# The first norm's sum of squares as four one-column matmuls, and its reciprocal root as a row by two DMAs

## The chip, the core and the metric

The kernel runs on one core of a Trainium2 chip. The metric is the device time of one execution in microseconds, on the one core used. A core has five engines that run their own instruction streams and meet only at semaphores: TensorE (PE in the rows, with PEld for its weight loads), VectorE (DVE), ScalarE (ACT), GpSimd (POOL) and SyncE (SP). DMAs are issued by SP and, at a few places, by ScalarE's queue.

## The reference, cut to what matters

Two layers of one encoder block; 512 tokens, 1024 features, everything float32. Each layer begins with an RMS norm whose output feeds one wide input projection and, through it, four branches; the last step of a layer adds a gated embedding to the residual stream. The part that the change touches is the first norm of each layer:

```
def rms_norm(x, g):
    xf = x.astype(jnp.float32)
    y = xf * lax.rsqrt(jnp.mean(xf * xf, axis=-1, keepdims=True) + EPS)
    return (y * g.astype(jnp.float32)).astype(x.dtype)

for i in range(DEPTH):
    h = rms_norm(x, norm_g[i])
    proj = h @ w_in[i]
    (a_u, a_v, a_z, b_x, b_z, c_q, c_kv, c_kr, c_z,
     d_q, d_k, d_v, d_z, gates) = jnp.split(proj, split_at, axis=-1)
    ... four branches, gated, summed, projected, added to x ...
```

`c_q`, `c_kv`, `c_kr` (the latents) and `a_v` are normed again by their own norms, so a factor per token in front of them cancels but for the small epsilon.

## The kernel before, in words

The residual stream `x` lies transposed: features on the 128 partitions, 8 tiles of 128 features, 512 tokens in the free dimension. Every weight matrix comes in chunks of 128 x 1024 numbers (8 blocks of 128 x 128) through a ring of four slots: SP loads `w_raw`, ScalarE rounds it to `w_hi` (line 971), GpSimd subtracts to get `w_lo` (lines 464, 466; VectorE does this for the first four chunks), and TensorE multiplies in three float32r passes, high by high, high by low, low by high (`mm3`, lines 491 to 493; `first_rows`, lines 541 to 556, for the first four chunks of layer 0). The chunk order is the list `chunk_order`. The order on each engine is written out by hand, one function per engine and stage, and all meeting points are semaphores.

The first stage of a layer, `front(l)`, exists once per engine:

- The squares of x's tiles are made by ScalarE (`gained`, `n_sq`) and added up by VectorE into `n_acc` (lines 1348, 1351), 128 x 512: per partition, the sum over the 8 feature tiles. `n_summed` counts the additions. In layer 1 this happens at the end of layer 0's `tail`.
- TensorE multiplies chunks `lat0` to `lat3` (latents, token rows on partitions, 448 columns, banks 0 to 3) with the unnormed input times the gain (`act_hi`, `act_lo`), then `av0` to `av3` (banks 4 to 7). The missing factor r per token, one over the root of the mean square, is put in afterwards. Each chunk holds two of the eight feature tiles; in layer 0 each tile of a latent chunk is three groups of four matmuls in `first_rows`.
- Between `lat3` and `av0`, `norm_total` (lines 560 to 566) multiplies a 128 x 128 matrix of ones with `n_acc`, split into `n_hi` and `n_lo`: every partition of bank 7 then holds the total of each of the 512 tokens. Block 3 of `av0` writes bank 7, and so waits for `n_root` (`taken`).
- ScalarE makes the square root of all of bank 7 into `r_b`, 128 x 512 (line 1008); a root of one number stands ahead of it (line 1006), and its table load with it. Then it squares the latents out of banks 0 to 3 (lines 1011, 1012, eight instructions, with their sums), rounds chunk `av2`, and takes the latents' root (line 1017).
- VectorE (lines 1408 to 1448) splits `n_acc`; in layer 0 takes the constants (`constants_taken`, lines 1357 to 1367) and makes the column of rope frequencies (line 1416, `freq_made`); gets r as a column, token on the partition, from `r_b` by a product with the identity and a reduction (lines 1419, 1421) and a reciprocal (1423); scales the latents out of PSUM (lines 1430 to 1436, `lat_taken`); in layer 0 waits for a transpose by TensorE (line 514, inside `av1`; it waits for `freq_made` and `lat_taken`) and computes the rope angles (lines 1445, 1372 to 1381); and makes the reciprocal of the whole `r_b` (line 1448).
- Then comes the loop over the 8 tiles: VectorE `n_t` = x times gain times `r_b` (line 1453), ScalarE rounds it to `h_hi` (line 1024), VectorE subtracts to `h_lo` (line 1336, `h_made`). TensorE's first product with h is `bx3`, right behind `av3`, and waits for `h_made` of each tile k in turn. All later input projections use h.

ScalarE's order in `front` is: `weights_up_to` for `lat3`, `av0`, `av1`, the roots, the squares, weights `av2`, the latents' root, then (after `av0` has ended) weights `av3`, (after `av1`) weights `bx3`, and the eight roundings of h.

## Time and profile before

| | us |
|---|---|
| time before, median of 3 runs | 1358.57 (1358.22 to 1361.79) |
| the profiled execution's own time | 1358.55 |
| its span in the profile | 1356.8 |
| TensorE busy | 1350.7 (6401 matmuls) |
| VectorE busy | 699.5 |
| ScalarE busy | 560.5 |
| GpSimd busy | 606.1 |

The profile is of one execution. Its span runs from the first to the last instruction, so the time around it is 1.75 us. The granted TensorE clock is full over the whole span. A timeline row gives the start, the busy time, and the instruction with what it writes and reads; a matmul's busy time overlaps the next one's, so what a matmul costs is read from the distance between two starts. Square brackets give idle time of the engine before the row and what ended it.

### The profile page before, as it was taken

What the parts mean: (1) busy time and instruction counts of PE and PEld (TensorE: products, weight loads), DVE (VectorE), ACT (ScalarE), POOL (GpSimd) and SP (SyncE); (2) the same over time, 40 slices, a digit from 0 to 9 for tenths busy, and PEclk for the clock granted to TensorE, in tenths of its full rate; (3) what the DMA queues carried; (4) which work ended last, traced back from release to release, by engine and by line L of the source; (5) the groups of instructions that cost most, each with busy time, mean ns of one, the idle gap of its engine ahead of it and who ended that gap; (6) DMA issues with size and microseconds to landing.
All of it is one profiled execution on the core that took longest, in us unless ns stands there. A gap on an engine that the chain in (4) does not pass through costs nothing.

```text
span 1356.8 us, 16150 instructions
## 1 busy us (share of the span) xinstructions
PE 1350.7 (100%) x6401; PEld 1136.3 (84%) x6401; DVE 699.5 (52%) x1065; ACT 560.5 (41%) x870; POOL 606.1 (45%) x455
## 2 busy tenths in 40 slices
PE   9999999999999999999999999999999999999998
PEld 8788888888888888888888888888888888888887
DVE  7996445144553223265779955441445432343743
ACT  6365454255552222224444554443555322222242
POOL 3444252444434445445565542334333444544543
PEclk9999999999999999999999999999999999999999
DMA  7322222222222333323333222223222333333332
GB/s 209 92 86 94 63 79 74 90 86 85 87 79 93 93 100 102 109 93 96 99 108 94 85 94 63 78 75 97 78 79 81 90 95 104 97 93 109 100 101 95
DMA packets 68268, 126.32 MB, mean 93 GB/s; under 512 B 9040, under 2 KB 37984, under 8 KB 68192
## 3 DMA queue, kind: packets, MB, share of 16 engines
q1 hardware_dynamic: 66960, 124.72, 30.2%
q8 instruction: 51, 0.84, 0.3%
q10 hardware_dynamic: 1232, 0.55, 0.1%
q14 instruction: 25, 0.20, 0.0%
HBM read 123.15 MB, written 2.10 MB: 92 GB/s over the span
## 4 chain that ended last, share of the span: by engine, by line
PE 98%; DVE 1%; ACT 0%; issue 0%; DVEq 0%
PE ps L491 31%; PE ps L493 31%; PE ps L492 31%; PE ps L764 1%; PE ps L699 1%; PE ps L800 1%; PE ps L686 1%; PE ps L541 1%; PE ps L551 0%; DVE n_t L1453 0%; PE ps L556 0%; DVE h_lo L1336 0%; PE ps L582 0%; DVE r_b L1448 0%; PE ps L618 0%
## 5 line engine op out<-in xcount | busy, mean ns | idle before, releaser
L464 POOL TENSOR_TENSOR w_lo<-w_raw,w_hi 128x512 fp32r<-128x512 f32 x222 | 304.4, 1371 | 724.4 <-ACT w_hi L971 724.3
L491 PE MATMUL ps<-h_hi,w_hi 128*128 128x512 f32 (+1 forms) x1160 | 452.6, 390 | 1.0 <-DVE h_lo L1336 1.0
L493 PE MATMUL ps<-h_hi,w_lo 128*128 128x512 f32 (+1 forms) x1160 | 450.2, 388 | 0.0
L492 PE MATMUL ps<-h_lo,w_hi 128*128 128x512 f32 (+1 forms) x1160 | 449.9, 388 | 0.0
L971 ACT ACTIVATE w_hi<-w_raw 128x1024 fp32r<-128x1024 f32 x227 | 238.6, 1054 | 172.5 <-PE ps L493 166.5
L466 POOL TENSOR_TENSOR w_lo<-w_raw,w_hi 128x512 fp32r<-128x512 f32 x222 | 303.7, 1368 | 0.0
L491 PEld LDWEIGHTS ps<-h_hi,w_hi 128*128 128x128 f32 x1160 | 217.9, 188 | 46.6 <-DVE h_lo L1336 2.6
L493 PEld LDWEIGHTS ps<-h_hi,w_lo 128*128 128x128 f32 x1160 | 217.8, 188 | 45.1
L492 PEld LDWEIGHTS ps<-h_lo,w_hi 128*128 128x128 f32 x1160 | 217.9, 188 | 43.3
L1771 DVE SCALAR_TENSOR_TENSOR m_part<-th,ps 128x512 f32<-128x512 f32 x48 | 33.0, 687 | 237.9 <-PE ps L493 237.7
L1196 ACT ACTIVATE th<-ps 128x512 f32<-128x512 f32 x48 | 28.7, 597 | 183.5 <-PE ps L493 183.5
L491 PE MATMUL ps<-act_hi,w_hi 128*128 128x512 f32 x192 | 75.2, 392 | 0.0
L493 PE MATMUL ps<-act_hi,w_lo 128*128 128x512 f32 x192 | 74.8, 389 | 0.0
L492 PE MATMUL ps<-act_lo,w_hi 128*128 128x512 f32 x192 | 74.7, 389 | 0.0
L491 PE MATMUL ps<-m_hi,w_hi 128*128 128x512 f32 x128 | 49.8, 389 | 0.0
L492 PE MATMUL ps<-m_lo,w_hi 128*128 128x512 f32 x128 | 49.8, 389 | 0.0
L493 PE MATMUL ps<-m_hi,w_lo 128*128 128x512 f32 x128 | 49.8, 389 | 0.0
L493 PEld LDWEIGHTS ps<-act_hi,w_lo 128*128 128x128 f32 x192 | 36.0, 188 | 7.6
L492 PEld LDWEIGHTS ps<-act_lo,w_hi 128*128 128x128 f32 x192 | 36.1, 188 | 7.3
L491 PEld LDWEIGHTS ps<-act_hi,w_hi 128*128 128x128 f32 x192 | 36.1, 188 | 7.3
L1596 DVE SCALAR_TENSOR_TENSOR merged<-th_b,ps 128x512 f32<-128x512 f32 x16 | 11.0, 684 | 50.9 <-PE ps L493 50.9
L491 PE MATMUL ps<-w_hi,act_hi 128*128 128x512 f32 (+1 forms) x96 | 36.9, 384 | 0.0
(329 smaller groups left out, 1992.2 us busy)
## 6 DMA issues: line engine op xcount, KB each, us to landing
w_raw<-w_in SPq DMA_DIRECT2D x180, 512.0 KB, 3.5
w_raw<-w_in SPq DMA_DIRECT2D x92, 128.0 KB, 2.5
w_raw<-w_in SPq DMA_DIRECT2D x36, 256.0 KB, 3.0
x<-x_in SPq DMA_DIRECT2D x8, 256.0 KB, 4.1
w_raw<-w_in SPq DMA_DIRECT2D x32, 64.0 KB, 2.0
out_x<-x SPq DMA_DIRECT2D x7, 256.0 KB, 3.7
p_raw<-p_in SPq DMA_DIRECT2D x2, 512.0 KB, 4.4
w_raw<-w_in ACTq DMA_DIRECT2D x4, 128.0 KB, 3.0
```

The source lines that it names most:

```text
L464: pool.tensor_tensor(w_lo_t[s][:, 0:4, :], w_raw_t[s][:, 0:4, :], w_hi_t[s][:, 0:4, :].bitcast(F32), ALU.subtract)
L466: pool.tensor_tensor(w_lo_t[s][:, 4:8, :], w_raw_t[s][:, 4:8, :], w_hi_t[s][:, 4:8, :].bitcast(F32), ALU.subtract).then_inc(w_lo_made, 1)
L491: pe.matmul(o, a_hi, b_hi, start=first, stop=False, skip_group_check=skip)
L492: pe.matmul(o, a_hi, b_lo, start=False, stop=False, skip_group_check=skip)
L493: return pe.matmul(o, a_lo, b_hi, start=False, stop=last, skip_group_check=skip)
L541: pe.matmul(bank(t, LAT), act_hi[:, at_[t]], v_hi[:, u, 0:LAT], start=k == 0, stop=False)
L686: last = pe.matmul(ps[:, s:s + keys], q[at_, b * P:keys], k[at_, 0:keys], start=False, stop=q is qr_lo, skip_group_check=True)
L699: last = pe.transpose(ps[:, o:o + P], prob[:, i:i + P], ident[:])
L764: last = pe.transpose(ps[:, b * 512 + t * P:b * 512 + (t + 1) * P], i, ident[:])
L971: act.activation(w_hi_t[s][:, 0:n, :], w_raw_t[s][:, 0:n, :], ACT.Copy).then_inc(w_hi_made, 1)
L1196: act.activation(th[:, i % 4, :], bank(b), ACT.Tanh, scale=0.5).then_inc(g_tanh, 1)
L1771: dve.scalar_tensor_tensor(o, th[:, i % 4, :], 1.0, bank(b), ALU.add, ALU.mult).then_inc(y_taken, 1)
```

## The change

TensorE no longer multiplies a matrix of ones with the split sums. It takes each block of 128 tokens of `n_acc` (plain float32) as the stationary operand and one column of ones as the moving one, four matmuls with one output column each, into columns 0 to 3 of bank 7 (`norm_sums`): the totals now lie with the token on the partition. It does this one step earlier: in layer 0 before the last feature tile of `lat3`, in layer 1 before `lat3`. VectorE turns the four columns into mean plus epsilon (`v`), ScalarE takes the root of 4 columns in place of 512, and VectorE the reciprocal r. `av0` now waits as a whole for `n_var`. The product with the identity, the reduction, the split, the first small root and the 512-column reciprocal are gone. In layer 0 VectorE does `constants_taken` after r in place of before it.

The row that the h loop needs, r of every token on all partitions, comes from memory: ScalarE's queue issues a DMA that writes r's 128 x 4 numbers to a scratch row of 512 (between the latents' squares and chunk `av2`), and, after chunk `av3` and a wait for the first one to land, a DMA that reads that row into all 128 partitions of `r_b`. VectorE waits for it where the reciprocal of `r_b` was.

```diff
--- before.py
+++ after.py
@@ -85,7 +85,7 @@
                      ("kn", 1), ("kr", 1))
 CC, CONSTS = columns(("ident", P), ("ones", P), ("negtri", P), ("neg_i", P), ("mask_c", P), ("mask_d", P),
                      ("keep", 1), ("inv_edge", G * PAD), ("inv_win", G), ("freq", 1))
-SM, SMALL = columns(("eps_v", TB), ("root", TB), ("r", TB), ("lat_sum", 2 * TB), ("lat_root", 2 * TB),
+SM, SMALL = columns(("v", TB), ("eps_v", TB), ("root", TB), ("r", TB), ("lat_sum", 2 * TB), ("lat_root", 2 * TB),
                     ("lat_inv", 2 * TB), ("bn", 6 * TB), ("mv", 2 * TB), ("ln_root", TB), ("ln_inv", TB),
                     ("kr_sum", TB), ("qk_sum", 16), ("qk_root", 16), ("qk_inv", 16), ("rq", 8), ("neg_rq", 8),
                     ("top", 8), ("bias", 8), ("total", 8), ("inv_total", 8), ("pool_gain", G), ("ln_col", 2 * G))
@@ -183,8 +183,7 @@
 
 
         xb, trail_a, trail_b = plan(0, 13, ("xb", [G, WIN], F32), ("trail_a", [WIN], F32), ("trail_b", [WIN], F32))
-        n_sq, n_acc, on_diag = plan(24, 32, ("n_sq", [2, SEQ], F32), ("n_acc", [SEQ], F32), ("on_diag", [SEQ], F32))
-        n_hi, n_lo = plan(24, 28, ("n_hi", [SEQ], F32R), ("n_lo", [SEQ], F32R))
+        n_sq, n_acc = plan(24, 32, ("n_sq", [2, SEQ], F32), ("n_acc", [SEQ], F32))
         cqn_hi, cqn_lo, ckvn_hi, ckvn_lo = plan(
             24, 36, ("cqn_hi", [2, SEQ], F32R), ("cqn_lo", [2, SEQ], F32R), ("ckvn_hi", [SEQ], F32R),
             ("ckvn_lo", [SEQ], F32R))
@@ -256,6 +255,8 @@
         def sems(names):
             return [sem(n) for n in names.split()]
 
+        r_row = nc.dram_tensor("r_row", (DEPTH, SEQ), F32).ap()
+
         x_loaded = [sem(f"x_loaded{d}") for d in range(KD)]
         pos_loaded, par_loaded, const_loaded, rows_loaded, p_loaded, out_stored = sems(
             "pos_loaded par_loaded const_loaded rows_loaded p_loaded out_stored")
@@ -267,8 +268,8 @@
 
         ones_made, consts_made, rope_args, rope_sines, freq_made, freq_ready, freq_taken = sems(
             "ones_made consts_made rope_args rope_sines freq_made freq_ready freq_taken")
-        hx_hi_made, hx_made, n_squared, n_summed, n_split, n_total, n_root = sems(
-            "hx_hi_made hx_made n_squared n_summed n_split n_total n_root")
+        hx_hi_made, hx_made, n_squared, n_summed, n_total, n_var, n_root, r_made, r_stored, rb_loaded = sems(
+            "hx_hi_made hx_made n_squared n_summed n_total n_var n_root r_made r_stored rb_loaded")
         gain_diag, gain_ready, gain_taken, h_scaled, h_hi_made, h_made = sems(
             "gain_diag gain_ready gain_taken h_scaled h_hi_made h_made")
         lat_squared, lat_var, lat_root, lat_scaled, lat_taken, lat_ready, lat_hi_made, lat_made = sems(
@@ -500,7 +501,7 @@
                                k == KD - 1)
                 last.then_inc(done(l, name), 1)
 
-            def project_rows(l, name, i, hi, lo, b, n=SEQ, rope_frequencies=False, taken=None):
+            def project_rows(l, name, i, hi, lo, b, n=SEQ, rope_frequencies=False):
 
                 w_hi, w_lo = chunk(l, name)
                 v_hi = w_hi[:].rearrange("p (k s) c -> p k (s c)", k=2)
@@ -518,8 +519,6 @@
                         s = slice(k * SEQ + t * P, k * SEQ + (t + 1) * P)
                         if l and k == 0 and name.startswith("lat"):
                             pe.wait_ge(x_moved, after((l - 1) * KD + 4 + t))
-                        if taken and k == 0 and t == TB - 1:
-                            pe.wait_ge(*taken)
                         last = mm3(bank(b + t, n), hi[:, s], lo[:, s], v_hi[:, u, 0:n], v_lo[:, u, 0:n], k == 0,
                                    k == KD - 1)
                 last.then_inc(done(l, name), 1)
@@ -531,6 +530,8 @@
                 v_lo = w_lo[:].rearrange("p (k s) c -> p k (s c)", k=2)
                 for u in range(2):
                     k = 2 * c + u
+                    if c == 3 and u:
+                        norm_sums(0)
                     at_ = [slice(k * SEQ + t * P, k * SEQ + (t + 1) * P) for t in range(TB)]
                     pe.wait_ge(hx_hi_made, after(k))
                     if c == 0 and u == 0:
@@ -557,13 +558,17 @@
                                          stop=k == KD - 1)
                 last.then_inc(done(0, f"lat{c}"), 1)
 
-            def norm_total(l):
-
-                pe.wait_ge(n_split, after(l))
-                if l:
+            def norm_sums(l):
+
+                pe.wait_ge(n_summed, after(l * KD + KD - 1))
+                if l == 0:
+                    pe.wait_ge(ones_made, after(0))
+                else:
                     pe.wait_ge(gate_scaled, after(l * KD - 1))
-                pe.matmul(bank(7), ones_r[:], n_hi[:], start=True, stop=False)
-                pe.matmul(bank(7), ones_r[:], n_lo[:], start=False, stop=True).then_inc(n_total, 1)
+                for t in range(TB):
+                    last = pe.matmul(ps[:, 7 * 512 + t:7 * 512 + t + 1], tile(n_acc, t, P), ones[:, 0:1], start=True,
+                                     stop=True)
+                last.then_inc(n_total, 1)
 
             def rope_rows(l):
 
@@ -594,9 +599,11 @@
                     if l == 0:
                         first_rows(i)
                         continue
+                    if i == 3:
+                        norm_sums(l)
                     project_rows(l, f"lat{i}", i, hx_hi, hx_lo, 0, LAT)
-                norm_total(l)
-                project_rows(l, "av0", 0, hx_hi, hx_lo, 4, taken=(n_root, after(l)))
+                pe.wait_ge(n_var, after(l))
+                project_rows(l, "av0", 0, hx_hi, hx_lo, 4)
                 project_rows(l, "av1", 1, hx_hi, hx_lo, 4, rope_frequencies=l == 0)
                 project_rows(l, "av2", 2, hx_hi, hx_lo, 4)
                 rope_rows(l)
@@ -1003,20 +1010,24 @@
                 weights_up_to(l, "av0")
                 act.wait_ge(*end_of(l, "lat2"))
                 weights_up_to(l, "av1")
-                act.activation(sm("root", 0), eps[:], ACT.Sqrt)
-                act.wait_ge(n_total, after(l))
-                act.activation(r_b[:], bank(7), ACT.Sqrt, bias=eps[:], scale=1.0 / D_MODEL).then_inc(n_root, 1)
+                act.wait_ge(n_var, after(l))
+                act.activation(sm("root"), sm("v"), ACT.Sqrt).then_inc(n_root, 1)
                 act.wait_ge(*end_of(l, "lat3"))
                 for t in range(TB):
                     act.activation(lat_sq[:, t, 0:2 * P], bank(t, 2 * P), ACT.Square, accum_out=sm("lat_sum", t))
                     last = act.activation(lat_sq[:, t, 2 * P:3 * P], ps[:, t * 512 + 2 * P:t * 512 + 3 * P], ACT.Square,
                                           accum_out=sm("lat_sum", TB + t))
                 last.then_inc(lat_squared, 1)
+                act.wait_ge(r_made, after(l))
+                act.dma_start(r_row[l].rearrange("(t p) -> p t", p=P), sm("r"), allow_slow_non_contiguous=True).then_inc(
+                    r_stored, 16)
                 weights_up_to(l, "av2")
                 act.wait_ge(lat_var, after(l))
                 act.activation(sm("lat_root"), sm("lat_sum"), ACT.Sqrt).then_inc(lat_root, 1)
                 act.wait_ge(*end_of(l, "av0"))
                 weights_up_to(l, "av3")
+                act.wait_ge(r_stored, 16 * after(l))
+                act.dma_start(r_b[:], r_row[l].partition_broadcast(P)).then_inc(rb_loaded, 16)
                 act.wait_ge(*end_of(l, "av1"))
                 weights_up_to(l, "bx3")
                 for k in range(KD):
@@ -1406,21 +1417,19 @@
                                   0.5, None, ALU.mult)
 
             def front(l):
-                dve.wait_ge(n_summed, after(l * KD + KD - 1))
-                settle(dve.tensor_copy(n_hi[:], n_acc[:]))
-                low(n_lo[:], n_acc[:], n_hi[:]).then_inc(n_split, 1)
+                dve.wait_ge(n_total, after(l))
+                dve.tensor_scalar(sm("v"), ps[:, 7 * 512:7 * 512 + TB], 1.0 / D_MODEL, EPS, ALU.mult, ALU.add).then_inc(
+                    n_var, 1)
+                dve.wait_ge(n_var, after(l))
+                dve.tensor_scalar(sm("eps_v"), sm("v"), EPS, None, ALU.mult)
+                dve.wait_ge(n_root, after(l))
+                dve.reciprocal(sm("r"), sm("root")).then_inc(r_made, 1)
                 if l == 0:
                     constants_taken()
                     gain_rows(0)
                     dve.wait_ge(pos_loaded, 16 * (TB + 1))
                     dve.tensor_scalar(freq_b[:], ones[:], freq[:, G:G + 1], None, ALU.mult).then_inc(freq_made, 1)
-                dve.wait_ge(n_root, after(l))
-                by_block = on_diag[:].rearrange("p (t s) -> p t s", t=TB)
-                settle(dve.tensor_tensor(by_block, r_b[:].rearrange("p (t s) -> p t s", t=TB),
-                                         over(ident[:], [P, TB, P], 1), ALU.mult))
-                settle(dve.tensor_reduce(sm("root"), by_block, AXIS_X, ALU.add))
-                dve.scalar_tensor_tensor(sm("eps_v"), sm("root"), EPS, sm("root"), ALU.mult, ALU.mult)
-                settle(dve.reciprocal(sm("r"), sm("root")))
+                dve.wait_ge(r_made, after(l))
                 dve.wait_ge(lat_squared, after(l))
                 dve.scalar_tensor_tensor(sm("lat_sum", 0, TB), sm("lat_sum", 0, TB), 1.0 / (2 * P), sm("eps_v"),
                                          ALU.mult, ALU.add)
@@ -1445,7 +1454,7 @@
                     dve.tensor_copy(freq_row[:], ps[:, FREQ_AT:FREQ_AT + HALF]).then_inc(freq_taken, 1)
                     dve.wait_ge(freq_taken, after(0))
                     rope_angles()
-                settle(dve.reciprocal(r_b[:], r_b[:]))
+                dve.wait_ge(rb_loaded, 16 * after(l))
                 for k in range(KD + 1):
                     if k < KD:
                         if k > 1:

```

## Rows read from the trace of the kernel before

**Rows 1.** The page's chain that ended last, shares of the span by engine.
```profile
PE 98%; DVE 1%; ACT 0%; issue 0%; DVEq 0%
```

**Rows 2.** TensorE's waits over the whole span: total, times, longest us.
```profile
PE ps L491 <- DVE h_lo L1336: 1.0, 3, 0.4
```

**Rows 3.** Timeline of TensorE, layer 0, product bx3: start us, busy us, what.
```profile
49.55 0.39 PE L491 MATMUL ps<-h_hi,w_hi 128*128 128x512 f32 x1
...
52.61 0.50 PE L491 MATMUL ps<-h_hi,w_hi 128*128 128x512 f32 x1 [0.18 <-DVE h_lo L1336]
...
56.98 0.39 PE L491 MATMUL ps<-h_hi,w_hi 128*128 128x512 f32 x1
```

**Rows 4.** Timeline of TensorE, layer 1, the same product.
```profile
723.27 0.39 PE L491 MATMUL ps<-h_hi,w_hi 128*128 128x512 f32 x1
...
728.71 0.39 PE L491 MATMUL ps<-h_hi,w_hi 128*128 128x512 f32 x1
```

**Rows 5.** Timeline of VectorE, layer 0, what starts the scaled input.
```profile
35.56 0.19 DVE L1445 COPY freq_row<-ps 128x32 f32<-128x32 f32 x1 [0.82 <-PE ps L514]
...
39.32 3.34 DVE L1448 RECIPROCAL r_b<-r_b 128x512 f32<-128x512 f32 x1
42.70 1.41 DVE L1453 SCALAR_TENSOR_TENSOR n_t<-x,par,r_b 128x512 f32<-128x512 f32 x2
...
54.65 1.47 DVE L1336 TENSOR_TENSOR h_lo<-n_t,h_hi 128x512 fp32r<-128x512 f32 x2
```

**Rows 6.** Timeline of TensorE, layer 0, last latent chunk and the norm's total.
```profile
24.04 0.99 PE L541 MATMUL ps<-w_hi,act_hi 128*128 128x448 f32 x4
...
26.52 0.40 PE L565 MATMUL ps<-n_hi,ones_r 128*128 128x512 f32 x1
```

**Rows 7.** Timeline of VectorE, last sum of squares in layer 0 and layer 1.
```profile
21.31 0.68 DVE L1351 TENSOR_TENSOR n_acc<-n_acc,n_sq 128x512 f32<-128x512 f32 x1
...
691.66 0.68 DVE L1351 TENSOR_TENSOR n_acc<-n_acc,n_sq 128x512 f32<-128x512 f32 x1
```

**Rows 8.** Timeline of TensorE, short matmuls: ten transposes, then one float32 product.
```profile
152.57 1.25 PE L699 MATMUL ps<-ident,prob 128*128 128x128 f32 x10
...
153.90 0.39 PE L492 MATMUL ps<-act_lo,w_hi 128*128 128x512 f32 x1
...
43.75 0.49 PE L576 MATMUL ps<-gain_d,ones 128*128 128x128 f32 x2
...
44.31 0.39 PE L492 MATMUL ps<-w_lo,act_hi 128*128 128x512 f32 x1
```

**Rows 9.** Timeline of ScalarE, layer 0, around the root of the norm.
```profile
25.33 1.28 ACT L1006 ACT_TABLE_LOAD   x1
...
30.20 1.11 ACT L971 ACTIVATE w_hi<-w_raw 128x1024 fp32r<-128x1024 f32 x1
```

**Rows 10.** Timeline of VectorE, layer 0, constants and latents.
```profile
25.05 0.21 DVE L1359 COPY ident<-c_st 128x128 f32<-128x128 f32 x1
...
28.85 0.68 DVE L1419 TENSOR_TENSOR on_diag<-r_b,ident 128x512 f32<-128x512 f32 x1
...
31.44 0.20 DVE L1430 RECIPROCAL small<-small 128x8 f32<-128x8 f32 x1 [0.63 <-ACT small L1017]
...
33.42 0.41 DVE L1436 TENSOR_TENSOR krs<-ps,small 128x256 f32<-128x256 f32 x1
```

**Rows 11.** DMA issues by line over the span: KB each, median us to landing.
```profile
pos_i<-pos_in SPq DMA_DIRECT2D x4, 0.5 KB, 3.1
```

**Rows 12.** Timeline of layer 1: ScalarE's two weight casts, VectorE's first and last h tiles.
```profile
704.10 1.12 ACT L971 ACTIVATE w_hi<-w_raw 128x1024 fp32r<-128x1024 f32 x1
...
706.54 1.06 ACT L971 ACTIVATE w_hi<-w_raw 128x1024 fp32r<-128x1024 f32 x1 [1.23 <-PE ps L493]
...
712.07 1.42 DVE L1453 SCALAR_TENSOR_TENSOR n_t<-x,par,r_b 128x512 f32<-128x512 f32 x2
...
725.90 1.48 DVE L1336 TENSOR_TENSOR h_lo<-n_t,h_hi 128x512 fp32r<-128x512 f32 x2
```


## The prediction

> **What bounds the kernel now.** I read the chain of work first: 98% of it is TensorE [rows 1]. So the time is TensorE's own work plus the places where it stands still, and a change that touches mostly other engines can give back no more than those. The list of TensorE's waits comes next; inside the kernel it names one releaser, VectorE's h_lo, three times, 1.0 us in total [rows 2]. The timeline shows where: in layer 0's product bx3, the first that uses the scaled input h. Its first matmul starts at 49.55 and the next product's at 56.98, so the eight tiles take 7.43 us [rows 3]. The same eight tiles in layer 1, where nothing is late, take 728.71 - 723.27 = 5.44 us, 0.68 a tile and 0.227 a matmul [rows 4]. The difference, 1.99 us, is the real price of these stalls (the slow matmul behind each gap counts too), and all that a faster path to h can win. Last I read VectorE's timeline backwards from there. The h loop starts at 42.70, right behind the reciprocal of the whole r_b, which begins at 39.32 and takes 3.34; ahead of that stand the rope angles, which started when TensorE's transpose (L514) released them at 35.56 [rows 5]. So in layer 0 TensorE's own position in av1 sets the start of the rope angles, and reciprocal and loop hang behind.
>
> **TensorE's own work, per layer.** Removed: two 512-column matmuls, 2 x 0.227 = 0.45 us. Added: four float32 matmuls of one output column. A float32 product that is no transpose is two instructions in this trace (L576, x2 for one call), so eight, each with its own 128-column weight load. No row shows one column. Ten transposes of 128 columns took 153.90 - 152.57 - 0.227 = 1.10 us, the changeover included: 0.11 each. The two pieces of L576 took 44.31 - 43.75 - 0.227 = 0.33 us: 0.17 each [rows 8]. Below 0.11 I don't go far, since the weight load is the same whatever is streamed; above, 0.17 has the right kind but 128 columns to stream. I take 0.11: 8 x 0.11 = 0.88, with 0.5 (pieces at half of that) and 1.36 as ends. Net +0.43 per layer, from +0.05 to +0.9; for two layers +0.86 (+0.1 to +1.8).
>
> **The new place of the sums.** They stand before the last feature tile in layer 0, which TensorE reaches at 24.04, and n_acc is whole at 21.31 + 0.68 = 21.99 [rows 6, 7]: no wait, 2 us to spare. In layer 1 they stand before lat3. I place that from rows: bx3 at 723.27, minus 96 matmuls of av0 to av3 (21.8), minus 0.6 for the small ones, minus 0.45, minus lat3's 24 at (26.52 - 24.04)/12 = 0.207, 5.0 us, gives 695.4; n_acc is whole at 692.34 [rows 4, 6, 7]. No wait, 3 us to spare. av0 now waits as a whole for n_var, but lat3's last tile (2.5 us) or all of lat3 (5 us) lies between, and VectorE has one 4-column instruction to do, so this costs nothing. If VectorE were busy there it would cost; it is not, its split of n_acc is gone.
>
> **The root.** The dummy root went, so the table load comes behind the wait for n_var. In layer 0 the totals are there about 25.0, ScalarE is free for the load at 25.33, 1.28 us long [rows 9], and the 4-column root and reciprocal end about 27.1. Squares of the latents wait for lat3's end (about 26.5 + 0.9 = 27.4) anyway, so the load is hidden. In layer 1 it has 5 us of lat3 over it. The row shows 1.28 us and the small root right behind it.
> The Trainium skill (ScalarE: Activation LUTs, What ACT_TABLE_LOAD costs) gives a load about 1380 ns of drain besides; this trace shows none at this place; by the rule r in layer 0 would come 1.4 us later, lat_taken (below) 1.2 later, and of its 1.5 us to spare 0.3 would be left, so that rival C would have 30% and not 10%.
>
> **VectorE in layer 0.** It took the constants at 25.05 to 28.85, 3.8 us, while the total and the root were made [rows 10]. Now it idles until r and takes them from 27.1 to 30.9. This is the part that is worse. What hangs on it is the latents' variance, then 31.1. But ScalarE is then in its cast of av2: the squares end at 27.4 + 2.4 = 29.8, the scratch write is issued (about 0.4), and the cast, 30.20 before [rows 9], now begins about the same and ends 31.3. The latents' reciprocal comes at 31.7 for 31.44, and lat_taken at 34.1 for 33.42 + 0.41 = 33.83 [rows 10]. TensorE asks for it at its transpose, which released freq_row at 35.56 [rows 5] and so stood at 35.2; with +0.43 it stands at 35.6. 1.5 us to spare: no cost. Gone with it are the product, reduction and split, which lay on no path here.
>
> **The h loop in layer 0.** Rope angles start with the transpose, 0.43 later, and end at 39.32 + 0.43 = 39.75. Then only rb_loaded is asked. The scratch write leaves about 30.2. The nearest row is a DMA of 4-byte elements, 128 of them: 3.1 us to landing [rows 11]; this one has 512. With 3.1 it lands at 33.3; ScalarE comes to its wait behind the cast of av3, about 34, issues the read, and by the same 3.1 it lands at 37.1: 2.6 us early. So the loop starts at 39.75 instead of 42.70, 2.95 earlier. Its last h_lo ended at 54.65 + 1.47 = 56.12 [rows 5] and now ends at 53.2; TensorE wants that tile at 49.55 + 0.43 + 7 x 0.68 = 54.7. 1.5 us of slack at the last tile, more at those before: all three stalls go, -1.99 us. What is late next is nothing up to bx2: the casts and splits for it hang on the same loop and on TensorE's own ends.
>
> **Layer 1.** There was no stall to win. The write leaves about 703.9, ahead of the cast that stood at 704.10, and lands by 707.0; the cast of av3 moves with TensorE from 706.54 to 707.0 and ends at 708.0, the read leaves and lands about 711.1. Before, the loop began at 712.07 and ended at 725.90 + 1.48 = 727.38; TensorE wanted the last tile at 723.27 + 7 x 0.68 = 728.03, now 728.46 [rows 4, 12]. So the loop may begin as late as 712.07 + 1.1 = 713.15; both DMAs together have 2 us to spare. Zero.
>
> **Sum.** -1.99 + 0.86 = -1.13 us. The profiled execution took 1358.55, which is the median of the runs (1358.57) within 0.02, so 1357.4. With the ends of the column matmuls: 1356.7 to 1358.4. A difference under 0.3% (4.1 us) can't be told from none by measurements of this kernel, so this is "no change" either way.
>
> **Rivals.**
> (A) *The DMA trip is slow and TensorE stalls behind it in layer 1* (slower). In the 3.1 us of the 128-element DMA, some part may grow with the count. Suppose, as an estimate, 1.1 of it does: 512 elements then take 2.0 + 4.4 = 6.4 us, the write lands at 710.3, the read at 713.4, and TensorE stalls 0.3 (limit 713.15); in layer 0 the read lands at 39.7, before its limit of 39.75 + 1.5 = 41.2. It decides from a trip (write plus read) over 713.15 - 703.9 = 9.2 us in layer 1 and 41.2 - 30.2 = 11.0 in layer 0, and the kernel is slower than before from 9.2 + 1.1 = 10.3. With 6.4 for each way the stalls are 3.6 and 1.8 us, and the time is 1358.55 - 1.13 + 5.4 = 1362.8. For it: elements of 4 bytes, nothing in the trace writes such, and the read also waits on ScalarE's queue. Against: the four 128-element copies in the trace landed in 3.1 us (median) [rows 11], and two such trips fit. Chance 12% that it costs over 1 us.
> The Trainium skill (DMA: Bandwidth & Descriptors, Rules for kernel authors) says a non-contiguous last dimension becomes one descriptor per element, and its Anatomy section that completion is the larger part of a fixed 2 us and worst when memory is the target; no run here shows a write of this kind yet, and by these the trip would be longer than two copies of 3.1.
> (B) *Column matmuls are dear*, 0.17 us a piece or more [rows 8]: +1.8 for two layers, 1358.4. For: they are the same kind. Against: nothing streams. 20%.
> (C) *The loop in layer 0 doesn't get earlier or meets something else*: VectorE's instructions double while GpSimd splits a chunk (in this loop one pair did), or constants or the write's issue on ScalarE push lat_taken past 35.6, and TensorE stands at its transpose. Then the 1.99 is kept in part or given back: about 1358.55 + 0.86 = 1359.4, and 1 us more for each us past the 1.5. 10%.
> (D) *The change does more than it says*: the gaps cost more than 1.99, or the earlier loop frees something later. TensorE has no other idle time inside, so under 1356 needs something the trace doesn't show. 4%.
> My forecast, 54%.
>
> **How the numbers follow.** The forecast's own range is 1356.7 to 1358.4; B ends there, C goes to 1359.4, A at its worst to 1362.8, and the runs of before scatter by 0.4 below and 3.2 above. Range 1356.0 to 1361.0. Faster by over 0.3% needs 1354.5, more than all stalls are worth: 2%. Slower by over 0.3%, over 1362.7, needs A at its worst or C by 4 us: 8%. No change: 90%.
>
> **What would show it.** In the changed kernel's trace: no wait of TensorE for h_lo, bx3 in layer 0 at 5.4 us between first matmul and bx2's; the eight one-column pieces within 0.9 us of TensorE's timeline; the table load behind n_var; rb_loaded not the releaser of VectorE's first n_t in layer 0 (the rope angles' last instruction is), and the releaser in layer 1 at about 711. Wrong it is if TensorE waits for lat_taken at the transpose, or for h_lo in layer 1, or if the sums' pieces take over 2 us.

## The result and the profile after

The changed kernel is slower: 1370.31 us (median of 6 runs, 1369.71 to 1371.35) against 1358.78 (6 runs of the kernel before on the same chip, 1358.22 to 1361.79). The ratio is 1.0082, 95% interval 1.0069 to 1.0095. The forecast was 1357.4, and the range ended at 1361.0. The profiled execution of after took 1369.71 with a span of 1367.9, 11.1 longer than before's 1356.8.

The page after: busy times, what the DMAs moved, the chain by engine and by line, and its two new DMAs (KB each, median us from issue to landing).
```profile
PE 1354.5 (99%) x6413; PEld 1138.6 (83%) x6413; DVE 683.6 (50%) x1057; ACT 559.1 (41%) x868; POOL 603.8 (44%) x455
...
PE 94%; DMA 3%; DVE 2%; SPq 0%; ACT 0%; issue 0%; ACTq 0%; DVEq 0%
PE ps L492 30%; PE ps L493 30%; PE ps L494 30%; DMA w_raw<-w_in 2%; DVE n_t L1462 1%; DVE h_lo L1347 1%; DMA r_b<-r_row 1%; PE ps L771 1%; PE ps L706 1%; PE ps L807 1%; PE ps L693 1%; DMA x<-x_in 0%; PE ps L542 0%; PE ps L557 0%; PE ps L552
...
r_b<-r_row ACTq DMA_DIRECT2D x2, 256.0 KB, 5.4
...
r_row<-small ACTq DMA_DIRECT2D x2, 2.0 KB, 9.6
```
VectorE lost 16 us of work and nothing came of it. In the chain TensorE fell from 98% [rows 1] to 94%, and two kinds of DMA came in: the new read, and, with more, the loads of weights. That second one no rival of the prediction had.

TensorE's waits, whole span, after (us in total, times, longest):
```profile
PE ps L492 <- DVE h_lo L1347: 4.9, 6, 1.6
PE ps L492 <- issue: 3.0, 2, 1.5
```
Before there were 1.0 us in three waits [rows 2]. The second row is a wait whose releaser the view doesn't name.

TensorE, bx3 in layer 0 (the first matmul, those behind a gap, and the first of bx2), then layer 1, against [rows 3, 4]:
```profile
52.30 0.47 PE L492 MATMUL ps<-h_hi,w_hi 128*128 128x512 f32 x1 [1.51 <-issue]
...
56.89 0.50 PE L492 MATMUL ps<-h_hi,w_hi 128*128 128x512 f32 x1 [1.59 <-DVE h_lo L1347]
...
61.26 0.39 PE L492 MATMUL ps<-h_hi,w_hi 128*128 128x512 f32 x1
...
729.75 0.47 PE L492 MATMUL ps<-h_hi,w_hi 128*128 128x512 f32 x1 [1.49 <-issue]
...
734.34 0.50 PE L492 MATMUL ps<-h_hi,w_hi 128*128 128x512 f32 x1 [1.62 <-DVE h_lo L1347]
...
737.12 0.79 PE L492 MATMUL ps<-h_hi,w_hi 128*128 128x512 f32 x1 [0.39 <-DVE h_lo L1347]
737.71 0.63 PE L493 MATMUL ps<-h_lo,w_hi 128*128 128x512 f32 x1
...
739.84 0.45 PE L492 MATMUL ps<-h_hi,w_hi 128*128 128x512 f32 x1
```
From the first matmul of bx3 to that of bx2 it is 8.96 us in layer 0 (7.43 before) and 10.09 in layer 1 (5.44 before). By the start of bx2 after is 4.28 us behind before in layer 0 (61.26 - 56.98) and 11.13 in layer 1 (739.84 - 728.71), and 11.1 is the whole difference of the spans. So all of it arises ahead of these two points.

ScalarE after, layer 0: the issue of the write (ACTq), the cast of av3, the issue of the read, the cast of bx3; then the same up to the read in layer 1.
```profile
29.02 0.45 ACTq L1022 DMA_DIRECT2D r_row<-small  x1
...
41.05 1.06 ACT L978 ACTIVATE w_hi<-w_raw 128x1024 fp32r<-128x1024 f32 x1 [9.15 <-DMA w_raw<-w_in]
41.08 0.34 ACTq L1030 DMA_DIRECT2D r_b<-r_row  x1
43.19 1.06 ACT L978 ACTIVATE w_hi<-w_raw 128x1024 fp32r<-128x1024 f32 x1 [1.07 <-DMA w_raw<-w_in]
...
706.64 0.37 ACTq L1022 DMA_DIRECT2D r_row<-small  x1
...
718.15 1.06 ACT L978 ACTIVATE w_hi<-w_raw 128x1024 fp32r<-128x1024 f32 x1 [8.62 <-DMA w_raw<-w_in]
718.18 0.34 ACTq L1030 DMA_DIRECT2D r_b<-r_row  x1
```
VectorE after: the rope angles' last instruction, the first tile of the loop in layer 0 and in layer 1, against [rows 5, 12].
```profile
39.50 0.23 DVE L1392 TENSOR_SCALAR turns<-turns 128x128 f32<-128x128 f32 x1
...
46.08 2.34 DVE L1462 SCALAR_TENSOR_TENSOR n_t<-x,par,r_b 128x512 f32<-128x512 f32 x2 [6.36 <-DMA r_b<-r_row]
...
724.10 1.77 DVE L1462 SCALAR_TENSOR_TENSOR n_t<-x,par,r_b 128x512 f32<-128x512 f32 x2 [11.24 <-DMA r_b<-r_row]
```
Read in order: the write leaves at 29.02 and takes 9.3 us to land. In that time SP's loads of weights hardly land either: the last of av3's four, issued at about 30, took 11.3 us, where it takes 3.6 in e17 below, whose write is quick. ScalarE was idle for 9.15 us ahead of the cast of av3, and that load ended the wait. Not all of the 9.15 is the write's: in e17 the same cast starts at 33.79, released by TensorE, so the write makes it 7.3 us late. The read stands behind that cast in ScalarE's order, leaves at 41.08, and lands 5.0 later. VectorE was ready at 39.73 and starts at 46.08. The same in layer 1, with the read leaving at 718.18. DMAs issued from 26 to 48 us, before and then after:
```profile
w_raw<-w_in SPq DMA_DIRECT2D x3, 512.0 KB, 3.4
w_raw<-w_in SPq DMA_DIRECT2D x4, 128.0 KB, 2.3
```
```profile
w_raw<-w_in SPq DMA_DIRECT2D x3, 512.0 KB, 5.7
w_raw<-w_in SPq DMA_DIRECT2D x4, 128.0 KB, 5.5
r_b<-r_row ACTq DMA_DIRECT2D x1, 256.0 KB, 5.0
r_row<-small ACTq DMA_DIRECT2D x1, 2.0 KB, 9.3
```

### The profile page after: what moved, and what is told of

Its sections match the earlier page's. It is cut to its first block, busy times and chain, and to the rows that moved or that the text cites. A ratio compares the mean times of both kernels' runs of the same rounds, so it can differ in the third digit from the quotient of the medians.

```text
span 1367.9 us, 16172 instructions
## 1 busy us (share of the span) xinstructions
PE 1354.5 (99%) x6413; PEld 1138.6 (83%) x6413; DVE 683.6 (50%) x1057; ACT 559.1 (41%) x868; POOL 603.8 (44%) x455
## 4 chain that ended last, share of the span: by engine, by line
PE 94%; DMA 3%; DVE 2%; SPq 0%; ACT 0%; issue 0%; ACTq 0%; DVEq 0%
PE ps L492 30%; PE ps L493 30%; PE ps L494 30%; DMA w_raw<-w_in 2%; DVE n_t L1462 1%; DVE h_lo L1347 1%; DMA r_b<-r_row 1%; PE ps L771 1%; PE ps L706 1%; PE ps L807 1%; PE ps L693 1%; DMA x<-x_in 0%; PE ps L542 0%; PE ps L557 0%; PE ps L552 0%; SPq L398 0%
## 5 line engine op out<-in xcount | busy, mean ns | idle before, releaser
L494 PE MATMUL ps<-w_hi,act_lo 128*128 128x512 f32 (+1 forms) x96 | 36.7, 382 | 0.0
```

What stands on the lines that cost most here:

```text
L494: return pe.matmul(o, a_lo, b_hi, start=False, stop=last, skip_group_check=skip)
```

## The experiments

Each line of results gives the median of the experiment, the median of before in the same job, and the ratio with its 95% interval. T in the expectations is the theory of the moment, R1 to R9 its rivals.

**Is it the write alone?** The kernel before with only the write added; nobody waits for it until the mix.
```diff
                 last.then_inc(lat_squared, 1)
+                act.wait_ge(r_made, after(l))
+                act.dma_start(r_row[l].rearrange("(t p) -> p t", p=P), sm("r"), allow_slow_non_contiguous=True).then_inc(
+                    r_stored, 16)
                 weights_up_to(l, "av2")
...
                 act.wait_ge(*end_of(l, "mix"))
+                act.wait_ge(r_stored, 16 * after(l))
```


> The kernel before, with the scratch write of r added behind the latents' squares; nobody waits for it until 'mix'. Theory T: the write of 512 elements of 4 bytes takes 9 to 10 us to land and weight loads issued while it runs land late with it, but TensorE only loses where somebody waits for the row or for a chunk that is due. Here r is ready some 1.5 us later than in the changed kernel, av3 is loaded ahead of it, and bx3's load has 10 us to spare: write lands after 9 to 10 us, chunk bx3 lands some us late, time within 1 us of before (1358.8). Rival R1: the write disturbs the weight loads so much that TensorE stalls whoever reads the row: 1362 or more.

1365.72 against 1358.62, 1.0048 (1.0033 to 1.0063). A 2 KB write in each layer that nobody needs costs 7 us. ScalarE in e1, the cast of bx3 and the first rounding of h:
```profile
42.99 1.06 ACT L974 ACTIVATE w_hi<-w_raw 128x1024 fp32r<-128x1024 f32 x1 [9.74 <-DMA w_raw<-w_in]
43.96 1.14 ACT L1030 ACTIVATE h_hi<-n_t 128x512 fp32r<-128x512 f32 x2
```
Here the load of bx3 was caught: it took 10.7 us to land, 3.4 before. Its cast came 4.7 us late (before, it stood at 38.26; the rest of the 9.74 is idle time that before has too), and it stands ahead of the roundings of h: VectorE started n_t on time at 42.73, and the loop ran late all the same. T had given this load 10 us to spare, up to TensorE's need of it, and had left out what ScalarE does behind its cast. So T fell, and the time is R1's.

**The change without the write.** The read takes an input row in place of the scratch; h is scaled by a wrong row.
```diff
-                act.wait_ge(r_made, after(l))
-                act.dma_start(r_row[l].rearrange("(t p) -> p t", p=P), sm("r"), allow_slow_non_contiguous=True).then_inc(
-                    r_stored, 16)
...
-                act.wait_ge(r_stored, 16 * after(l))
-                act.dma_start(r_b[:], r_row[l].partition_broadcast(P)).then_inc(rb_loaded, 16)
+                act.dma_start(r_b[:], rows_in[l, 2].partition_broadcast(P)).then_inc(rb_loaded, 16)
```


> The changed kernel without the write: the row DMA reads 512 numbers of an input into r_b, so h is scaled by the wrong row (that part of the computation is left out). The column matmuls and the read stay. Theory T: the weight loads land on time again (chunk av3 cast at 35, not 41), the read is issued about 35 and lands within 4 us, ahead of the end of the rope angles (39.7); no wait for h_lo and none at the gain in either layer; time = before + 0.9 for the columns - 2.0 for layer 0's old stalls = 1357.7. Rival R3: the read into 128 partitions is the slow part: it stays near 1368.

1358.21 against 1358.62, 0.9996 (0.9986 to 1.0005). No wait for h_lo is left, the loop starts at 39.32. R3 fell with it: the read took 5.3 us and cost nothing. So the loss is the write's, and the rest of the change is worth what the forecast gave it, within what can be measured.

**The write in larger pieces.** e3: 128 pieces of 16 B (r's four numbers of a partition side by side, so the row's tokens are permuted against h). e6: the whole change, with r first transposed by TensorE to 4 rows of 128, so that the write has 4 pieces of 512 B; nothing is left out or permuted (VectorE copies `ident` ahead of the sums for it).
```diff
--- e3
-                act.dma_start(r_row[l].rearrange("(t p) -> p t", p=P), sm("r"), allow_slow_non_contiguous=True).then_inc(
+                act.dma_start(r_row[l].rearrange("(p t) -> p t", t=TB), sm("r")).then_inc(
...
--- e6
+                pe.wait_ge(r_made, after(l))
+                pe.transpose(ps[0:TB, 7 * 512:7 * 512 + P], sm("r"), ident[:]).then_inc(rt_ready, 1)
...
+                dve.tensor_copy(r_t[0:TB, :], ps[0:TB, 7 * 512:7 * 512 + P]).then_inc(rt_taken, 1)
...
+                act.dma_start(r_row[l].rearrange("(t p) -> t p", p=P), r_t[0:TB, :]).then_inc(
...
```


> The changed kernel with the same 2 KB written as 128 pieces of 16 bytes, one per partition, instead of 512 of 4 bytes (the row's tokens are then permuted, so h is scaled in the wrong order). Theory T, cost by the number of elements: 9.6 us become 2 + 7.6/4 = 4 us, the write lands about 33, chunk av3 is hardly late, the stalls go: about 1358. Rival R2: it is any small write to memory: lands after 9 to 10 us again, time near 1370.

> The changed kernel, whole, with r's column first turned by TensorE into 4 rows of 128 (one transpose per layer) and written as 4 pieces of 512 bytes. Theory T (cost by the number of small pieces written): the write lands in 2 to 3 us, no load is late, the read lands before the rope angles end, no wait of TensorE for h_lo: before - 2.0 + 0.9 + 0.3 = 1357.8. Rival R2 (any write into memory and reading it back is slow): 1364 or more.

e3: 1358.46 against 1358.62, 0.9991 (0.9982 to 1.0001), write 3.0 us, read 4.5. e6: 1358.24 against 1358.73, 0.9997 (0.9988 to 1.0006). Both times came as T said; its reason, the count of pieces, falls further down (e9). The view has no landing time for e6's write; its read left at 33.30, 4.8 us behind the write. TensorE in e6, first matmul of bx3 and of bx2, and VectorE's first tile:
```profile
50.18 0.39 PE L494 MATMUL ps<-h_hi,w_hi 128*128 128x512 f32 x1
...
55.89 0.40 PE L494 MATMUL ps<-h_hi,w_hi 128*128 128x512 f32 x1
...
39.59 2.45 DVE L1470 SCALAR_TENSOR_TENSOR n_t<-x,par,r_b 128x512 f32<-128x512 f32 x2
```
bx3 takes 5.71 us where it took 7.43: the gaps that the prediction wanted gone are worth 1.72, and it had said 1.99.

**Where the read stands.** The read and its wait ahead of the cast of av3.
```diff
+                act.wait_ge(r_stored, 16 * after(l))
+                act.dma_start(r_b[:], r_row[l].partition_broadcast(P)).then_inc(rb_loaded, 16)
                 act.wait_ge(*end_of(l, "av0"))
                 weights_up_to(l, "av3")
-                act.wait_ge(r_stored, 16 * after(l))
-                act.dma_start(r_b[:], r_row[l].partition_broadcast(P)).then_inc(rb_loaded, 16)
```


> The changed kernel with the wait for the write and the read issued ahead of the cast of chunk av3 on ScalarE. Theory T: the write lands at 38.5 and the read leaves then, not at 41.1 behind the cast that waits for its late weights; h starts 2 to 3 us earlier in each layer, if the read itself isn't slower beside the delayed weight loads; the cast of av3 still comes at 41. Time 1370.3 - 5 = 1365. Rival R4: the read is held by the backlog of weight loads, not by ScalarE's order: it lands at 46 as before, time 1370.

1366.72 against 1358.62, 1.0054 (1.0039 to 1.0069), between T's 1365 and R4's 1370. The write left at 29.90 there, 0.88 later than in after. From its issue to the start of the loop it is 44.82 - 29.90 = 14.9 us, in after 17.06: the place in the queue is worth 2.1 us in layer 0, so R4 fell; the slow write and the read are the rest.

**Count, size or neighbours?** Four DMAs of 128 elements (e8); one of 128 neighbouring elements (e9, whose read repeats that row four times); the same 128 elements 64 B apart (e10); 256 pieces of 8 B (e11); all 512 elements 64 B apart (e17). e9, e10, e11 and e17 scale h by a wrong or permuted row.
```diff
--- e8
+                for t in range(TB):
+                    act.dma_start(r_row[l, t * P:(t + 1) * P].rearrange("(p u) -> p u", u=1), sm("r", t)).then_inc(
+                        r_stored, 16)
...
--- e9
+                act.dma_start(r_row[l, 0:P].rearrange("(p u) -> p u", u=1), sm("r", 0)).then_inc(
... (the read repeats this row four times)
--- e10
+        r_row = nc.dram_tensor("r_row", (DEPTH, P, 16), F32).ap()
...
+                act.dma_start(r_row[l, :, 0:1], sm("r", 0), allow_slow_non_contiguous=True).then_inc(
...
+                act.dma_start(r_b[:], rows_in[l, 2].partition_broadcast(P)).then_inc(rb_loaded, 16)
--- e11
+                act.dma_start(r_row[l].rearrange("(a p b) -> p a b", a=2, b=2), sm("r").rearrange("p (a b) -> p a b", a=2)).then_inc(
...
--- e17
+        r_row = nc.dram_tensor("r_row", (DEPTH, P, TB, 16), F32).ap()
...
+                act.dma_start(r_row[l, :, :, 0:1], sm("r").unsqueeze(2), allow_slow_non_contiguous=True).then_inc(
...
+                act.dma_start(r_b[:], rows_in[l, 2].partition_broadcast(P)).then_inc(rb_loaded, 16)
```


> The changed kernel with the write as four DMAs of 128 elements of 4 bytes, one per block of 128 tokens. Same 512 elements. Theory T: the elements themselves are slow to write, so the last lands after 9 to 10 us and the time stays at 1370. Rival R6: it is the form of the one DMA (partition by 4 strided elements): four plain ones land in 3 us each, as the 128-element loads of positions did, time 1358.

> The changed kernel with only the first 128 tokens' r written (128 elements of 4 bytes) and the row repeated four times by the read (tokens 128 to 511 are scaled wrongly: that part is left out). Theory T, cost proportional to the elements of 4 bytes: the write lands in 3.5 to 4 us, time near 1358. Rival R7: a fixed price of writes below some size, however few: 9 us, 1370.

> The run with 128 elements of 4 bytes, but each element written 64 bytes from the next (and the row read from an input, so h is scaled by the wrong row: that part is left out). Theory C (neighbouring 4-byte pieces of one memory line are written one behind the other): apart they land in about 3 us, and the time is near 1358. Theory S (a piece of 4 bytes is slow by itself, however many and wherever): 8.4 us again, weight loads late, about 1366.

> The changed kernel with the 2 KB written as 256 pieces of 8 bytes (tokens permuted). 512 pieces of 4 bytes took 9.6 us, 128 of 16 took 3.0, 128 of 4 took 8.5. If the count of pieces decided: (9.6 + 3.0)/2, about 5 us. If the size of a piece: between 3 and 9 according to where the step lies; theory S with a step at 4 bytes says 3 to 4 us, and 1358.

> The changed kernel with all 512 numbers of r still written as 4-byte pieces, but each piece 64 B from the next in memory; the read takes an input row in place of the scratch (h is then scaled by the wrong row; the time is what is wanted). Theory C (neighbouring 4-byte pieces in one stretch of memory are written one behind another, and that is what takes 9.6 us): the write lands in 2.4 to 4 us, weight loads around 30 us land in 3.5 to 5 us, TensorE has no wait for h_lo over 0.5 us, time 1358.0 to 1359.0. Theory N (with as many as 512 pieces the count decides, and the spaced write of 128 was quick only because it was short): four times 2.4, the write lands in 7 to 10 us and the time is 1363 or more.

| write | pieces | lands after, us (median) | time, us | before, us |
|---|---|---|---|---|
| after | 512 x 4 B, neighbours | 9.6 | 1370.31 | 1358.78 |
| e8 | 4 DMAs of 128 x 4 B, neighbours | 7.8 each | 1368.55 (2 runs) | 1358.73 |
| e9 | 128 x 4 B, neighbours | 8.5 | 1370.73 (2 runs) | 1358.73 |
| e11 | 256 x 8 B, neighbours in one half | 4.7 | 1360.24 (1 run) | 1358.76 |
| e3 | 128 x 16 B | 3.0 | 1358.46 (10 runs) | 1358.62 |
| e17 | 512 x 4 B, 64 B apart | 3.6 | 1358.27 (11 runs) | 1358.45 |
| e10 | 128 x 4 B, 64 B apart | 2.4 | 1358.49 (1 run) | 1358.76 |

Four DMAs in place of one (e8, rival R6) didn't help. T, "proportional to the count", fell with e9: a quarter of the elements took 8.5 us (e9's time can't be held against the others', since its read, in pieces of 512 B, took 9.5 us too). What decides is seen by e17 against after: the same queue, source, count and size of pieces, only their places in memory differ, and the write lands in 3.6 us for 9.6. (e17's read takes an input row, but it leaves at 33.80, when the write has landed.) It is nearness of pieces under 16 B: neighbours of 8 B took 4.7 us, of 16 B 3.0. e10 and e11 are one execution each. DMAs issued from 26 to 48 us in e17, to be held against the last fence of the section before:
```profile
w_raw<-w_in SPq DMA_DIRECT2D x3, 512.0 KB, 3.5
w_raw<-w_in SPq DMA_DIRECT2D x4, 128.0 KB, 2.6
r_b<-rows_in ACTq DMA_DIRECT2D x1, 256.0 KB, 4.6
r_row<-small ACTq DMA_DIRECT2D x1, 2.0 KB, 3.2
```
With the pieces apart, the loads of weights land as they did before. In e17 ScalarE's cast of av3 stands behind TensorE again, not behind a load, to be held against its row at 41.05 in after:
```profile
33.79 1.06 ACT L978 ACTIVATE w_hi<-w_raw 128x1024 fp32r<-128x1024 f32 x1 [1.84 <-PE ps L494]
```
e17's ratio is 0.9998 (0.9989 to 1.0007). That neighbouring small pieces are written one behind another inside the memory or the DMA engine is our reading; the runs show that nearness decides, not the reason inside. All these writes left from ScalarE's queue; what one from SP's queue does to the loads was not tried.
The Trainium skill (DMA: Bandwidth & Descriptors, Specifications) says that below 512 B the DMA engine does a read-modify-write, and (same page, Issuing engines are not separate DMA queues) that DMAs issued by different engines run on the same 16 DMA engines and interleave. The first would fit neighbours that wait for each other, but size alone, which is its rule, did not cost here: 4-byte pieces apart took 2.4 to 3.6 us. That the queues share engines fits: behind e1's write from ScalarE's queue a load of SP's took 10.7 us for 3.4. That they interleave doesn't show: from 32.0 to 38.3 in after, with loads of 512 KB under way, 16 GB/s were moved, 85 in before.

**The wait at bx3's start.** After waits 1.5 us in each layer before its first matmul of bx3. That matmul overwrites bank 2, and VectorE copies the gains out of that bank inside the loop, at k = 3 (51.92 + 0.28 = 52.20, bx3 at 52.30). e7: the copy ahead of the loop. It was run twice, the second time beside the changed kernel once more.
```diff
+                dve.wait_ge(gain_ready, after(l))
+                dve.tensor_copy(sm("ln_col"), ps[:, 2 * 512 + P:2 * 512 + P + 2 * G])
+                dve.tensor_copy(gain_row[:].rearrange("p q a c -> p (q a c)"), bank(2, P)).then_inc(
+                    gain_taken, 1)
                 dve.wait_ge(rb_loaded, 16 * after(l))
                 for k in range(KD + 1):
...
-                    if k == 3:
-                        dve.wait_ge(gain_ready, after(l))
...
```


> The changed kernel with the copy of the gains, for which TensorE waits at the start of bx3, ahead of the h loop and not at its fourth tile. Theory T (h_lo of the last tiles sets the end of bx3; the 1.5 us wait at its start only shifts the stall): bx3 starts 1.5 us earlier and ends 0 to 0.3 later, 1370.5. Rival R8: the two waits add up, and 1.5 us per layer come back: 1367.5.

> The changed kernel once more, beside the one with the gains copied early, on one chip. Both theories: 1370. If the run with early gains is then 3 us faster again, the two waits of bx3 do add up (R8); if this one is at 1368 too, the 3 us were the chip's or the write's scatter (T).

> The changed kernel with the copy of the gains ahead of the h loop, once more. Rival R8 (early gains give back the 1.5 us wait in each layer): 1367.5, 3 us under the changed kernel beside it. Theory T (the last h_lo sets the end of bx3; only the 0.3 us of the two copies leave the loop): within 1 us of the changed kernel beside it.

e7: 1367.56 against 1358.76, then 1370.47 against 1358.83 (1.0083, 1.0069 to 1.0097). The changed kernel again, beside the second: 1368.16 (1.0067, 1.0053 to 1.0081). The two runs contradict each other by 2.9 us, so the times alone don't decide between T and R8; one reason is the clock: behind the last wait for h_lo in layer 0 of the second profile two tiles took 1.39 and 1.28 us for 0.68. The rows of layer 0 where the clock was full do decide. From the end of the loop's first two n_t to the first matmul of bx2 it is 59.52 - 46.84 = 12.7 us in e7's first profile, 61.26 - 48.42 = 12.8 in after, and 60.84 - 48.14 = 12.7 in after again. So the early wait gives back 0.2 at most, not 1.5: TensorE starts bx3 earlier and stands longer inside it (2.2 and 2.4 us for h_lo, in after 1.6), because the last h_lo sets bx3's end.

**Can the 1.99 us be had without the trip?** Three tries on the kernel before: rope angles behind the h loop (e5), the angles later still, behind `norm_low(3)` (e12), the reciprocal ahead of the wait for the transpose (e14).
```diff
--- e5, e12: out of their place behind line 1445, to behind the loop / behind norm_low(3)
-                    dve.wait_ge(freq_taken, after(0))
-                    rope_angles()
--- e14
+                settle(dve.reciprocal(r_b[:], r_b[:]))
                 if l == 0:
                     dve.wait_ge(freq_ready, after(0))
```


> The kernel before, with layer 0's rope angles (3.9 us of VectorE) behind the h loop in place of ahead of it; no column matmuls, no DMA. Theory T (the 1.99 us of bx3 in layer 0 hang on the start of the h loop): the loop starts near 38.9, bx3 takes 5.4 us, TensorE waits for nothing, time = before - 2.0 = 1356.7. Rival R5: the angles then delay the layer norm behind them, or the loop collides elsewhere, and the 2 us come back as a later wait: 1358.6.

> The kernel before, with layer 0's rope angles taken out from ahead of the h loop and put behind the last split of the normed v (some 50 us later), where the casts of weights no longer wait behind VectorE. No column matmuls, no DMA. Theory T: the h loop starts near 39.5 and not 42.7, the stalls of bx3 in layer 0 (1.99 us) go, and nothing comes back: before - 2.0 = 1356.8. Rival R5 (as in the run with the angles right behind the loop, where they came back as a 3.6 us wait): VectorE is nearly full up to 112 us, and 3.9 us more there make TensorE wait for the mixing or for branch B: 1358.6 or more.

> The kernel before with the reciprocal of r_b moved ahead of VectorE's wait for the transpose of the rope frequencies in layer 0 (nothing else). Theory T: of its 3.34 us 0.8 fall into VectorE's idle time there, so the h loop starts 0.8 us earlier in layer 0 (42.70 to 41.9), the last h_lo with it; of the 1.99 us of stalls in bx3 0.8 go: 0.8 us below before, 1357.9. Rival R9 (the reciprocal now runs beside GpSimd's split and doubles, or the gaps in bx3 stay because the next wait is just behind): within 0.3 us of before.

All three missed. e5: 1362.63 against 1358.73, 1.003 (1.0019 to 1.0041). bx3 was as hoped (0.3 us of waits), but the angles doubled beside GpSimd's splits (their 0.95 us instruction took 2.90), what VectorE does behind them came late (ckvn_lo at 81.90 for 78.91), and TensorE stood for it here, in e5's timeline:
```profile
82.74 0.51 PE L491 MATMUL ps<-w_hi,ckvn_hi 128*128 128x512 f32 x1 [3.58 <-issue]
```
e12: 1359.09 against 1358.76, 1.0002 (0.9993 to 1.0011), the gain spent in four waits of 0.3 to 0.6 us. e14: 1359.0 against 1358.45, 1.0005 (0.9996 to 1.0014). The reciprocal ran at 34.40 to 37.75, but then the angles lay beside GpSimd's split at 39.01 and 40.25, and the loop began at 42.83 where it had begun at 42.70:
```profile
39.07 3.00 DVE L1378 SCALAR_TENSOR_TENSOR ang<-turns,ang 128x128 f32<-128x128 f32 x3
```

**The row without permuting h.** With 16-byte pieces the row's order is (p t), so the loop must read `r_b` with a stride of four numbers. e15 is the changed kernel so, e16 the kernel before with only the row so; both compute all.
```diff
+                act.dma_start(r_row[l].rearrange("(p t) -> p t", t=TB), sm("r")).then_inc(
...
-                        dve.scalar_tensor_tensor(n_t[:, k % 2, :], tile(x, k), col(l, "norm", k), r_b[:], ALU.mult,
-                                                 ALU.mult).then_inc(h_scaled, 1)
+                        dve.scalar_tensor_tensor(n_t[:, k % 2, :].rearrange("q (t p) -> q t p", t=TB),
+                                                 tile(x, k).rearrange("q (t p) -> q t p", t=TB), col(l, "norm", k),
+                                                 r_b[:].rearrange("q (p t) -> q t p", t=TB), ALU.mult,
+                                                 ALU.mult).then_inc(h_scaled, 1)
```


> The kernel before, whole, with its sums and its way to r unchanged, but the row by memory in place of the 3.3 us reciprocal: r's column written as 128 pieces of 16 bytes, and the h loop reading the row in that order by a strided view. Theory T (4-byte pieces beside each other were the fault, not the trip): the write lands in 3 us, the read near 38.5, the h loop starts near 39.5 in place of 42.7 and TensorE has no work added: before - 2.0 = 1356.8. Rival: the strided view of r_b slows each n_t, or the read lands after 41 us: 1358.7 or more.

> The changed kernel, whole, with pieces of 16 bytes and the strided view. Theory T: as the run with 16-byte pieces and permuted tokens, 1358.4: before - 2.0 + 0.9 for the column matmuls = 1357.7, and 0.9 over the run without these matmuls beside it.

e16: 1364.96 against 1358.83, 1.0045 (1.0032 to 1.0057). e15: 1365.22, 1.0049 (1.0035 to 1.0063). A miss with a cause: the trip was quick (write 1.4, read 4.9 in e16) and the loop began early, but a tile of n_t took longer. VectorE in e16, then in e3, whose row is contiguous:
```profile
41.19 3.22 DVE L1461 SCALAR_TENSOR_TENSOR n_t<-x,par,r_b 128x512 f32<-128x512 f32 x2
...
45.05 1.14 DVE L1461 SCALAR_TENSOR_TENSOR n_t<-x,par,r_b 128x512 f32<-128x512 f32 x1
```
```profile
44.13 0.75 DVE L1462 SCALAR_TENSOR_TENSOR n_t<-x,par,r_b 128x512 f32<-128x512 f32 x1
```
TensorE uses a tile in 0.68 us, the loop makes one in 0.75 + 0.68; it lives by its head start, and the longer n_t eats 0.39 us of that in each of the eight tiles, 3.1 in all. TensorE waits for h_lo 3.4 us in e15 and 4.0 in e16, in e3 0.3. bx3 takes 10.1 us in layer 0 and 7.9 in layer 1 in e16 (7.43 and 5.44 before), which is 5.2 of the 5.5 us by which its span is longer than before's; a part of that is again the clock, granted 0.57 from 57 to 60 (e15: 0.50 from 57 to 63).
The Trainium skill (SBUF — State Buffer, Door 1: The DMA port swizzle) says that lines in SBUF are 16 bytes and every access that crosses to a new one pays; a stride of four float32 numbers is 16 bytes, and the trace agrees in direction (1.14 us for 0.75); the edit also gives x and n_t three-dimensional views, and the two were not tried apart.

No version is measurably better than the kernel before. The best that computes all is e6, 1358.24 against 1358.73, within the interval.

## Why the prediction was wrong

The difference of the spans, +11.1 us, by the prediction's own steps, each from the distance between two rows of TensorE in both traces:

| step | forecast | measured |
|---|---|---|
| start, up to the sums (24.04 to 24.69) | 0 | +0.65 |
| column matmuls, layer 0 and 1 | +0.43, +0.43 | +0.44, +0.54 |
| the h loop in layer 0 | -1.99 | +3.20 |
| layer 1 | 0 | +6.30 |
| sum | -1.13 | +11.13 |

The first row is scatter and not the change: TensorE waited 0.5 us for `act_hi` at 12.43, ahead of all that was changed, and that wait is between 0 and 0.9 us in the other profiles.

**The step that failed** is the trip in "The h loop in layer 0" and "Layer 1": "the nearest row is a DMA of 4-byte elements, 128 of them: 3.1 us to landing ... with 3.1 it lands at 33.3". That row [rows 11] is a read from memory; the change's DMA is a write to memory with neighbouring 4-byte pieces, which took 9.3 us in layer 0 and 10.0 in layer 1, and e9 shows that even 128 such pieces take 8.5. The read, at 5.0 and 5.8, is also over the 3.1, and cost nothing where no slow write was in its way (e2, e6). The second half of the failed step is that the write's effect on other loads stood at nothing. e1 and e2 are the proof from both sides: the write alone costs 7 us, and without it the time is 1358.2.

**The limits, held against the rows.** The prediction's limits for the read say when stalls begin; their size needs two more terms. In layer 0 the limit was 41.2, with the late start 41.9, and the read landed at 46.08, 4.2 late. The loop then took 0.9 us longer than before (46.08 to 60.40, before 42.70 to 56.12). TensorE lost 1.67 ahead of bx3 and 8.96 - 5.44 = 3.52 in it, 5.19. In layer 1, 713.15 has the 0.43 of layer 0's columns in it; with the measured delay, 4.83 (717.47 to 722.30 at the gains' product), in its place the limit is 712.07 + 0.65 + 4.83 = 717.55. The read landed at 724.10, 6.55 late; the loop took 1.56 less than before (13.75 for 15.31), and the clock cost about 1.3 (last section): 6.3, and the measured loss is 6.30. A limit worked out so is of use where a price is missing, but e1 shows what it doesn't cover: a load that is held up costs, though nobody waits for the row.

**What the prediction did not see.** First, that the write would hold others: it had only the row's own users wait for it. The cast of av3 came 7.3 us late for want of its weights, and the read is queued behind that cast, so the read left 2.7 us after the write had landed. The question "what does this DMA share with the loads around it" was asked of ScalarE's queue only. Second, bx3 waits for the gains' copy inside the loop; hardly a loss of its own (e7), but a wait at a place where the prediction had none. Third, TensorE's clock, which fell behind the stalls and cost about 1.3 us in layer 1 (last section).

**The rivals.** A was the right side and, for the read, the right place; 12% was too little. Its price was: with 6.4 us each way it gave 1362.8, since it let the 3.1 us of a read grow with the count. The trip took 46.08 - 29.02 = 17.06 us and 724.10 - 706.64 = 17.46, not 12.8. The count that it went by hardly mattered (e9), and it left out the loads of weights. The Trainium skill (DMA: Bandwidth & Descriptors, Rules for kernel authors) has one descriptor per element for such a write, which stood beside A and pointed the right way; but e17 has as many elements as after and lands in 3.6 us. The fixed 2 us that the prediction takes from the same page stands there for DMAs that GpSimd issues; these are ScalarE's. B fell: eight pieces took 25.50 - 24.69 = 0.81 us, 0.10 each for 0.11 forecast. C did not happen: VectorE had lat_taken at 34.3, TensorE's transpose released it at 36.65, and the angles ended at 39.73, forecast 39.75. That match is luck: they started 0.66 later than forecast (36.65 for 35.99) and took 0.8 less than before. D did not happen: without the slow write the gaps were worth 1.72 (e6), not more than 1.99.

**Right, by the rows**: no wait at the sums; the table load beside lat3's last tile, with the small root right behind it.
```profile
24.69 0.95 PE L569 MATMUL ps<-ones,n_acc 128*128 128x1 f32 x8
25.50 1.07 PE L542 MATMUL ps<-w_hi,act_hi 128*128 128x448 f32 x4
...
25.20 1.28 ACT L1014 ACT_TABLE_LOAD   x1
26.50 0.21 ACT L1014 ACTIVATE small<-small 128x4 f32<-128x4 f32 x1
```
The root follows its table load by 0.02 us (26.50 - 26.48); the drain of about 1380 ns in the Trainium skill (ScalarE: Activation LUTs, What ACT_TABLE_LOAD costs) doesn't show in after either. The constants behind r took 26.83 to 29.42, 2.6 us for the 3.8 forecast.

The range failed by its method: both ends of the unseen write came from one kind of row, a read, and 6.4 us, an estimate from it, was rival A's value and its worst at once.

## What to carry to other kernels

A kind of transfer that the trace doesn't show has no nearest row (here a write in neighbouring 4-byte pieces; the trace had reads in such pieces and writes in large ones): give it its own range, and ask for each new DMA which loads share its path and which in-order engine waits for those. Numbers that lie across the partitions should go to memory in pieces of 16 B or more, or apart from each other (512 neighbouring 4-byte pieces took 9.6 us, the same pieces 64 B apart 3.6); if the order suits the reader, as in e6, the copy behind it is free, and a strided operand instead can cost more than the trip (1.14 for 0.75 us a tile). Work moved into idle time of VectorE must be checked for what GpSimd does in that time, at the place it lands and at that of what it pushes (e5, e14).
